# Per head means of squares of the sliding window attention's queries and keys: small fp32 matmuls and transposes, or two dense matmuls in split precision

## The chip, the cores and the metric

One core of a Trainium2 chip runs the whole program. The metric is the time of one execution on the device in microseconds; smaller is better.

## The reference, cut to what matters

A hybrid layer (gated linear attention beside sliding window attention, then a gated MLP) and two layers of another model follow each other on one sequence of 512 tokens with model width 1024. The change touches one step of the first layer: the RMS normalisation of each head's query and key in the sliding window attention, 8 query heads and 2 key heads of 64 elements.

```python
def rms_norm(x, g):
    xf = x.astype(jnp.float32)
    y = xf * lax.rsqrt(jnp.mean(xf * xf, axis=-1, keepdims=True) + EPS)
    return (y * g.astype(jnp.float32)).astype(x.dtype)
...
    h = rms_norm(x, mix_norm)
    z = h @ w_in
    gq, gk, gv, gr, glr, sq, sk, sv = split_cols(z, SPLITS)
...
    sq = rms_norm(sq.reshape(B, L, SWA_HEADS, SWA_HD), q_norm)
    sk = rms_norm(sk.reshape(B, L, SWA_KV_HEADS, SWA_HD), k_norm)
    sv = sv.reshape(B, L, SWA_KV_HEADS, SWA_HD)
    o_swa = swa_sink_attention(sq, sk, sv, sinks).astype(dt)
```

## The kernel before

Activations lie with the features on the 128 partitions and the 512 tokens along the free axis. Each engine has a program of its own, written out in order by hand; semaphores join them, and nothing reorders them.

**Split precision.** Every large product runs as fp32r matmuls on split operands. A weight tile of 128x1024 lands in `stage`; ScalarE copies it to `w_hi` (`split_hi`, called `split(t)`, L1346), GpSimd subtracts to get `w_lo` (`split_lo`, L422, four instructions of 128x256). TensorE then runs 24 matmuls of 128x512 into one of two PSUM banks: 16 with `w_hi` (against `xn_hi` and `xn_lo`), 8 with `w_lo` (against `xn_hi`). `stage`, `w_hi` and `w_lo` have two buffers each. ScalarE splits tile t + 2 in its round t; GpSimd's split of tile t + 1 waits for ScalarE's split of it (`hi_ready`) and for tile t - 1 on TensorE (`tile_done`).

**The input projection.** Tiles 0 to 3 are another form. Tiles 4 to 17 run in the loop `for t in range(N_GV, N_IN)` on TensorE: `dense(T_IN, t, a, b)` issues matmuls a to b of the 24, and `at_0`, `at_8`, `at_12` and `at_16` put other work between them (at the tile's start, after 8, after 12, after 16). VectorE and ScalarE have loops with the same t. VectorE's `project(t - 1)` (L2015) scales a finished tile out of its bank into `z`.

**The normalisation.** The five tiles that hold keys (index 0) and queries (1 to 4) are handled in rounds `SUMS_AT = [5, 6, 9, 11, 13]`. For index i: ScalarE squares the tile into `tmp` (`swn_square`, L1441). TensorE sums the squares by four fp32 matmuls with the squares as stationary operand and two columns of a constant as moving one (`swn_sums`, L716, at `at_12`), which gives 8 columns, tokens on the partitions. ScalarE takes Ln and Exp of the 8 columns (`swn_root`, L1446, L1447), VectorE makes a Newton step on them and spreads them to 128x512 (`swn_newton`, L2020 to L2023), TensorE transposes that back by four transposes (`swn_spread`, L724, at `at_0` of a later round), and VectorE multiplies the tile by it (`swn_scale`, L2029). `MB` is the PSUM bank all this goes through.

**What stands around it.** ScalarE's round 5 holds, after the root of index 0, the gate chain of the linear attention (L1551, L1552, L1554), then `split(7)`. Its round 6 holds square and root of index 1, `decays(0)`, `split(8)`. VectorE's round 6 holds `log_decay(0)` and `log_decay(1)`, each a tensor_tensor (L2033), a scan (L2035) and a tensor_tensor (L2038), all from SBUF. At `at_0(7)` TensorE makes tables from the bias (L831, L832). The queries' and keys' scores come at `at_16` of rounds 7, 8, 10 to 15 (L666), the attention's transposes at L678.

## Time and profile before

| | |
|---|---|
| median of 3 runs | 1754.53 us (1753.83 to 1754.73) |
| profiled execution, its own time | 1754.19 us |
| span of its trace | 1752.4 us |
| busy in the span | TensorE 1736.8, VectorE 826.6, ScalarE 751.9, GpSimd 979.3 us |
| mean granted clock of TensorE | 0.999 of full speed |

The span runs from the first to the last instruction of the trace; the execution's own time has 1.8 us around it. Times in the trace are counted from the span's start. Matmuls overlap, so the distance between the starts of two of them is what one costs, not its length.

### The profile page before, as it was taken

Reading aid. Unit: us, or ns where it says so; the run is one execution under the profiler, and the core shown is the slowest. Engines: PE = TensorE matmul, PEld = TensorE weight load, DVE = VectorE, ACT = ScalarE, POOL = GpSimd, SP = SyncE. Lnnn points to the kernel's source line nnn. Section 1 sums busy time; section 2 is a strip of 40 time slices with the busy share of each in tenths; the row PEclk is TensorE's granted clock in tenths of the full one; section 3 lists DMA queues with packets and bytes.
Section 4 is the critical chain, followed back from the end, with each engine's and each line's share of the span. In section 5 each row is a group of like instructions: output and inputs, shape, how many; then the busy total and the mean of one; then the engine's idle time right before and its main releaser. Section 6 shows DMA issues by size and latency. Waiting matters only on the chain.

```text
span 1752.4 us, 25481 instructions
## 1 busy us (share of the span) xinstructions
PE 1736.8 (99%) x8358; PEld 1413.3 (81%) x8358; DVE 826.6 (47%) x1611; ACT 751.9 (43%) x1226; POOL 979.3 (56%) x1176
## 2 busy tenths in 40 slices
PE   8999999999999999999999999999999999999998
PEld 6777788888888778888888888877777888888887
DVE  4764655555311455566232323567677551414143
ACT  4455555555322444435232323346565542323243
POOL 5433655555555434357575757755554675757574
PEclk9999999999999999999999999999999999999999
DMA  5221223332323322222232322323331333332232
GB/s 189 70 67 61 84 98 96 96 96 96 96 96 138 105 67 82 73 85 96 96 96 96 96 96 96 138 81 106 108 108 50 96 95 98 96 96 96 96 96 96
DMA packets 48484, 167.41 MB, mean 96 GB/s; under 512 B 5328, under 2 KB 6624, under 8 KB 48384
## 3 DMA queue, kind: packets, MB, share of 16 engines
q1 hardware_dynamic: 48032, 165.83, 29.1%
q8 instruction: 43, 0.70, 0.2%
q10 hardware_dynamic: 384, 0.67, 0.1%
q14 instruction: 25, 0.20, 0.0%
HBM read 164.24 MB, written 2.24 MB: 95 GB/s over the span
## 4 chain that ended last, share of the span: by engine, by line
PE 97%; ACT 1%; DVE 1%; issue 0%; DMA 0%; POOL 0%; SPq 0%; DVEq 0%; POOLq 0%; ACTq 0%
PE bank L620 19%; PE bank L518 13%; PE bank L519 13%; PE bank L524 13%; PE bank L928 5%; PE bank L929 5%; PE bank L933 5%; PE bank L971 2%; PE bank L977 2%; PE bank L972 2%; PE bank L638 2%; PE bank L639 2%; PE bank L644 2%; PE bank L1194 1%; PE bank L1223 1%; PE bank L1206 1%
## 5 line engine op out<-in xcount | busy, mean ns | idle before, releaser
L422 POOL TENSOR_TENSOR w_lo<-stage,w_hi 128x256 fp32r<-128x256 f32 x1128 | 926.3, 852 | 715.3 <-ACT w_hi L1346 408.5
L1346 ACT ACTIVATE w_hi<-stage 128x1024 fp32r<-128x1024 f32 x282 | 298.0, 1057 | 480.8 <-PE bank L519 337.6
L518 PE MATMUL bank<-xn_hi,w_hi 128*128 128x512 f32 x544 | 211.7, 389 | 0.0
L519 PE MATMUL bank<-xn_lo,w_hi 128*128 128x512 f32 x544 | 211.6, 389 | 0.0
L518 PE MATMUL bank<-arena,w_hi 128*128 128x512 f32 x496 | 192.9, 389 | 0.0
L519 PE MATMUL bank<-arena,w_hi 128*128 128x512 f32 x496 | 192.9, 389 | 0.0
L620 PE MATMUL bank<-xn_hi,w_hi 128*128 128x512 f32 x464 | 190.3, 410 | 0.0
L620 PE MATMUL bank<-xn_lo,w_hi 128*128 128x512 f32 x464 | 182.0, 392 | 0.0
L928 PE MATMUL bank<-xn_hi,w_hi 128*128 128x512 f32 x352 | 136.9, 389 | 0.0
L929 PE MATMUL bank<-xn_lo,w_hi 128*128 128x512 f32 x352 | 136.9, 389 | 0.0
L524 PE MATMUL bank<-xn_hi,w_lo 128*128 128x512 f32 x544 | 135.0, 389 | 0.0
L524 PE MATMUL bank<-arena,w_lo 128*128 128x512 f32 x496 | 132.6, 389 | 0.0
L1895 DVE TENSOR_TENSOR x<-x,bank 128x512 f32 x48 | 33.0, 688 | 210.8 <-PE bank L524 210.8
L2609 DVE TENSOR_TENSOR tmp<-tmp,rstd 128x512 f32<-128x512 f32 x64 | 46.0, 718 | 170.8 <-ACT tmp L1867 170.5
L620 PE MATMUL bank<-xn_hi,w_lo 128*128 128x512 f32 x464 | 123.7, 399 | 0.0
L519 PEld LDWEIGHTS bank<-xn_lo,w_hi 128*128 128x128 f32 x544 | 102.1, 188 | 21.2
L524 PEld LDWEIGHTS bank<-xn_hi,w_lo 128*128 128x128 f32 x544 | 102.1, 188 | 21.2
L518 PEld LDWEIGHTS bank<-xn_hi,w_hi 128*128 128x128 f32 x544 | 102.1, 188 | 21.1
L518 PEld LDWEIGHTS bank<-arena,w_hi 128*128 128x128 f32 x496 | 93.1, 188 | 19.4
L524 PEld LDWEIGHTS bank<-arena,w_lo 128*128 128x128 f32 x496 | 93.1, 188 | 19.3
L519 PEld LDWEIGHTS bank<-arena,w_hi 128*128 128x128 f32 x496 | 93.1, 188 | 19.3
L620 PEld LDWEIGHTS bank<-xn_hi,w_hi 128*128 128x128 f32 x464 | 87.2, 188 | 26.3 <-issue 9.9
(331 smaller groups left out, 2827.4 us busy)
## 6 DMA issues: line engine op xcount, KB each, us to landing
stage<-weights SPq DMA_DIRECT2D x283, 512.0 KB, 3.4
bias<-table SPq DMA_DIRECT2D x11, 896.0 KB, 5.3
out<-z SPq DMA_DIRECT2D x8, 256.0 KB, 2.1
x<-x_in SPq DMA_DIRECT2D x3, 512.0 KB, 7.8
bias<-swa_table SPq DMA_DIRECT2D x4, 256.0 KB, 4.5
con<-consts SPq DMA_DIRECT2D x1, 640.0 KB, 10.0
bias<-table SPq DMA_DIRECT2D x5, 128.0 KB, 3.5
stage<-weights ACTq DMA_DIRECT2D x2, 256.0 KB, 4.1
```

The lines of the kernel that those rows point to most:

```text
L422: ins = nc.gpsimd.tensor_tensor(w_lo[:, p_, ks], stage[:, p_, ks], w_hi[:, p_, ks].bitcast(F32), ALU.subtract)
L518: pe.matmul(G[p_][:], w_hi[:, p_, k], hi[:, k], start=(first and k == ks[0]), stop=False)
L519: mm = pe.matmul(G[p_][:], w_hi[:, p_, k], lo[:, k], start=False, stop=False)
L524: mm = pe.matmul(G[p_][:], w_lo[:, p_, k], hi[:, k], start=False, stop=(last and k == ks[-1]))
L620: mm = pe.matmul(G[p_][:], (w_hi if i < 2 * KD else w_lo)[:, p_, k], (xn_lo if i < 2 * KD and i % 2 else xn_hi)[:, k], start=(i == 0), sto ...
L638: pe.matmul(G[dd][:], w, ff_hi[:, k], start=(k == k0), stop=False)
L639: mm = pe.matmul(G[dd][:], w, ff_lo[:, k], start=False, stop=False)
L928: pe.matmul(UP[bank][:], w_hi[:, p_, k], xn_hi[:, k], start=(k == 0), stop=False)
L929: mm = pe.matmul(UP[bank][:], w_hi[:, p_, k], xn_lo[:, k], start=False, stop=False)
L933: mm = pe.matmul(UP[bank][:], w_lo[:, p_, k], xn_hi[:, k], start=False, stop=(k == KD - 1))
L1346: act.activation(w_hi[:, p_], stage[:, p_], ACT.Copy).then_inc(hi_ready, 1)
L2609: dve.tensor_tensor(tmp[:, 2 + p_], tmp[:, p_], rstd[:], ALU.mult).then_inc(u_ready, 1)
```

## The change

The sums go by two dense fp32r matmuls of 128x512 with a block diagonal matrix `mean_h` (1/64 within each head's 64 rows): the squares are split in a high part (ScalarE, Copy into `swn_split[:, 0]`) and a low part (GpSimd, `swn_low`), as in every large product. The result has the mean of each head already spread over its 64 partitions, so nothing is transposed. ScalarE's root works on 128x512 (Ln, Exp, and the square of the result), and the Newton step becomes part of VectorE's scaling, three operations of 128x512 in place of three small or spreading ones and one; the factor -0.5 goes into the norms' weights at the start. The pair of matmuls stands at `at_16`, where the sums stood at `at_12`. GpSimd's loop over tiles is written out, with `swn_low` behind the split of the next tile. The copy that makes `mean_r` moves to the opening. Cut to its core:

```diff
@@ -145,6 +145,7 @@
         mean_r = sb("mean_r", [P, P], F32R)
+        mean_h = sb("mean_h", [P, P], F32R)
@@ -154,6 +155,7 @@
         square_split = zr[:, 16:18]
+        swn_split = zr[:, 12:14]
         y = z[:, 0:KD].rearrange("p k s -> p (k s)").rearrange("p (h k s) -> p h k s", h=2, k=KD)
@@ -434,10 +435,18 @@
-            with pool.Fori(1, T_OUT // 2 + 1) as m:
-                for p_ in range(2):
-                    split_lo(m, p_)
-            split_lo(T_OUT // 2 + 1, 0)
+            def swn_low(i):
+
+                pool.wait_ge(swn_hi, i + 1)
+                if i:
+                    pool.wait_ge(swn_ss, i)
+                nc.gpsimd.tensor_tensor(swn_split[:, 1], tmp[:, i % 2], swn_split[:, 0].bitcast(F32),
+                                        ALU.subtract).then_inc(swn_lo, 1)
+
+            for t in range(2, T_OUT + 3):
+                split_lo(t // 2, t % 2)
+                if t - 1 in SUMS_AT:
+                    swn_low(SUMS_AT.index(t - 1))
             gla_low(0)
@@ -708,21 +717,14 @@
-            def swn_sums(i):
-
-                pe.wait_ge(swn_sq, i + 1)
+            def swn_means(i):
+
+                pe.wait_ge(mean_ready, 2)
                 pe.wait_ge(*((swn_done, i) if i else (rstd_ready, 1)))
-                for t in range(NQ):
-                    mm = pe.matmul(MB[:, 2 * t:2 * t + 2], tmp[:, i % 2, t * P:(t + 1) * P], ccol("mean_64")[:, 0::64],
-                                   start=True, stop=True)
-                mm.then_inc(swn_ss, 1)
-
-            def swn_spread(i):
-
-                pe.wait_ge(swn_found, i + 1)
-                for t in range(NQ):
-                    mm = pe.transpose(MB[:, t * P:(t + 1) * P], tmp[:, i % 2, t * P:(t + 1) * P], ident)
-                mm.then_inc(swn_turned, 1)
+                pe.wait_ge(swn_hi, i + 1)
+                pe.matmul(MB[:], mean_h[:], swn_split[:, 0], start=True, stop=False)
+                pe.wait_ge(swn_lo, i + 1)
+                pe.matmul(MB[:], mean_h[:], swn_split[:, 1], start=False, stop=True).then_inc(swn_ss, 1)
@@ -821,10 +823,7 @@
-                if t == 6:
-                    swn_spread(0)
-                elif t == 7:
-                    swn_spread(1)
+                if t == 7:
                     pe.wait_ge(buckets_in, 16)
@@ -835,14 +834,8 @@
                     token_major(1)
-                elif t == 10:
-                    swn_spread(2)
                 elif t == 11:
                     token_major(2)
-                elif t == 12:
-                    swn_spread(3)
-                elif t == 14:
-                    swn_spread(4)
                 if t in TURN_AT:
@@ -862,14 +855,14 @@
             def at_12(t):
-                if t in SUMS_AT:
-                    swn_sums(SUMS_AT.index(t))
                 if t == 16:
             def at_16(t):
+                if t in SUMS_AT:
+                    swn_means(SUMS_AT.index(t))
                 if t in TURN_AT:
@@ -1437,14 +1430,21 @@
                 if i >= 2:
-                    act.wait_ge(swn_turned, i - 1)
+                    act.wait_ge(swn_done, i - 1)
                 act.activation(tmp[:, i % 2], z[:, SWN_TILES[i]], ACT.Square).then_inc(swn_sq, 1)
+                act.wait_ge(swn_sq, i + 1)
+                if i:
+                    act.wait_ge(swn_ss, i)
+                act.activation(swn_split[:, 0], tmp[:, i % 2], ACT.Copy).then_inc(swn_hi, 1)
                 act.wait_ge(swn_ss, i + 1)
-                link("act", act, act.activation(swn_y, MB[:, 0:8], ACT.Ln, bias=eps_col))
-                act.activation(swn_y, swn_y, ACT.Exp, scale=-0.5).then_inc(swn_r, 1)
+                if i:
+                    act.wait_ge(swn_done, i)
+                link("act", act, act.activation(rstd_h[:], MB[:], ACT.Ln, bias=eps_col))
+                link("act", act, act.activation(rstd_h[:], rstd_h[:], ACT.Exp, scale=-0.5))
+                act.activation(tmp[:, i % 2], rstd_h[:], ACT.Square).then_inc(swn_r, 1)
@@ -1525,6 +1525,9 @@
             act.activation(glr_w[:, :, 0:16], pcol("w_glr").rearrange("p (k c) -> p k c", k=KD), ACT.Copy).then_inc(glr_split, 1)
+            act.wait_ge(con_in, 16)
+            act.activation(mean_r[:], ccol("mean_d"), ACT.Copy).then_inc(mean_ready, 1)
+            act.activation(mean_h[:], ccol("mean_64"), ACT.Copy).then_inc(mean_ready, 1)
             split(4)
@@ -1558,7 +1561,6 @@
                     act.activation(lam_s[:, 2:4], lam_s[:, 0:2], ACT.Exp).then_inc(lam_exp, 1)
-                    act.activation(mean_r[:], ccol("mean_d"), ACT.Copy).then_inc(mean_ready, 1)
                     act.wait_ge(tab_sb, 3)
@@ -2002,6 +2004,8 @@
                               glr_w[:, :, 0:16].bitcast(F32), ALU.subtract).then_inc(glr_split, 1)
+            both = par[:, _cols["q_norm"][0]:_cols["k_norm"][1]]
+            dlink(dve.tensor_scalar(both, both, -0.5, None, ALU.mult))
             dve.tensor_scalar(neg_sinks, pcol("sinks"), -1.0, None, ALU.mult).then_inc(sink_negated, 1)
@@ -2014,19 +2018,15 @@
-            def swn_newton(i):
+            def swn_scale(i):
                 dve.wait_ge(swn_r, i + 1)
-                dlink(dve.scalar_tensor_tensor(out=swn_a, in0=MB[:, 0:8], scalar=EPS, in1=swn_y, op0=ALU.add, op1=ALU.mult))
-                dlink(dve.scalar_tensor_tensor(out=swn_b, in0=swn_a, scalar=-0.5, in1=swn_y, op0=ALU.mult, op1=ALU.mult))
-                wide = [v.rearrange("p (g o) -> p g o", o=1).broadcast_to([P, 8, 64]) for v in (swn_b, swn_y)]
-                dve.scalar_tensor_tensor(out=tmp[:, i % 2].rearrange("p (g d) -> p g d", g=8), in0=wide[0], scalar=1.5, in1=wide[1],
-                                         op0=ALU.add, op1=ALU.mult).then_inc(swn_found, 1)
-
-            def swn_scale(i):
-                dve.wait_ge(swn_turned, i + 1)
                 zi, g = z[:, SWN_TILES[i]], pcol("q_norm" if i else "k_norm")
-                dve.scalar_tensor_tensor(out=zi, in0=zi, scalar=g, in1=MB[:], op0=ALU.mult, op1=ALU.mult).then_inc(swn_done, 1)
+                dve.scalar_tensor_tensor(out=zi, in0=zi, scalar=g, in1=rstd_h[:], op0=ALU.mult, op1=ALU.mult)
+                dlink(dve.scalar_tensor_tensor(out=tmp[:, i % 2], in0=MB[:], scalar=eps_col, in1=tmp[:, i % 2],
+                                               op0=ALU.add, op1=ALU.mult))
+                dve.scalar_tensor_tensor(out=zi, in0=tmp[:, i % 2], scalar=-3.0, in1=zi, op0=ALU.add,
+                                         op1=ALU.mult).then_inc(swn_done, 1)
@@ -2138,7 +2138,6 @@
                 if t == 5:
-                    swn_newton(0)
                     for j in range(2):
@@ -2146,7 +2145,6 @@
                     log_decay(0)
-                    swn_newton(1)
                     log_decay(1)
@@ -2176,8 +2174,6 @@
                     scale(SCORE_AT.index(t - 1))
-                if t in SUMS_AT[2:]:
-                    swn_newton(SUMS_AT.index(t))
                 if t in SCORE_AT:
```

TensorE in rounds 5 to 7 of the loop, before: the end of tile 6 and what follows. L620 are the tile's matmuls, L716 the sums, L724 the transposes, L831 and L832 the tables.

```order
L620 MATMUL bank<-xn_lo,w_hi 128x512
L716 MATMUL bank<-con,tmp 128x2 [waits swn_done,swn_sq]
L716 MATMUL bank<-con,tmp 128x2 x3
L620 MATMUL bank<-xn_hi,w_hi 128x512
L620 MATMUL bank<-xn_lo,w_hi 128x512
L620 MATMUL bank<-xn_hi,w_hi 128x512
L620 MATMUL bank<-xn_lo,w_hi 128x512
L620 MATMUL bank<-xn_hi,w_lo 128x512 [waits lo_ready]
L620 MATMUL bank<-xn_hi,w_lo 128x512 x7
L724 MATMUL bank<-con,tmp 128x128 [waits swn_found]
L724 MATMUL bank<-con,tmp 128x128 x3
L831 MATMUL bank<-ff_space,par 16x512 [waits gate_log,buckets_in]
```

The same place after (L629 are the tile's matmuls, L725 and L727 the new pair, L830 the tables):

```order
L629 MATMUL bank<-xn_hi,w_hi 128x512
L629 MATMUL bank<-xn_lo,w_hi 128x512
L725 MATMUL bank<-arena,mean_h 128x512 [waits swn_hi,swn_done,mean_ready]
L727 MATMUL bank<-arena,mean_h 128x512 [waits swn_lo]
L629 MATMUL bank<-xn_hi,w_lo 128x512 [waits lo_ready]
L629 MATMUL bank<-xn_hi,w_lo 128x512 x7
L830 MATMUL bank<-ff_space,par 16x512 [waits gate_log,buckets_in]
```

The pair stands after the sixteenth matmul and not after the twelfth, waits for a second engine, and the transposes are gone.

GpSimd after, from the w_lo split of tile 5 to that of tile 8 (L423 the splits, L443 the low part of the squares):

```order
L423 TENSOR_TENSOR w_lo<-stage,w_hi 128x256 x3
L423 TENSOR_TENSOR w_lo<-stage,w_hi 128x256 [waits tile_done,hi_ready]
L423 TENSOR_TENSOR w_lo<-stage,w_hi 128x256 x3
L443 TENSOR_TENSOR arena<-tmp,arena 128x512 [waits swn_hi]
L423 TENSOR_TENSOR w_lo<-stage,w_hi 128x256 [waits tile_done,hi_ready]
L423 TENSOR_TENSOR w_lo<-stage,w_hi 128x256 x3
L443 TENSOR_TENSOR arena<-tmp,arena 128x512 [waits swn_ss,swn_hi]
L423 TENSOR_TENSOR w_lo<-stage,w_hi 128x256 [waits tile_done,hi_ready]
```

Before, the same stretch was a loop of the splits alone; the two L443 are new, each behind the split of the tile that comes after the one whose pair needs it.

ScalarE before, from the root of index 0 to that of index 1 (L1346 is the w_hi split of tile 7):

```order
L1446 ACTIVATE small<-bank,small 128x8 [waits swn_ss]
L1447 ACTIVATE small<-small 128x8 [waits act_chain]
L1551 ACTIVATE qkv<-bank,par 128x512 [waits gate_abs,gate_in]
L1552 ACTIVATE qkv<-qkv 128x512 [waits act_chain]
L1551 ACTIVATE qkv<-bank,par 128x512 [waits gate_abs,gate_in,act_chain]
L1552 ACTIVATE qkv<-qkv 128x512 [waits act_chain]
L1554 ACTIVATE qkv<-qkv 128x512 [waits act_chain]
L1554 ACTIVATE qkv<-qkv 128x512
L1346 ACTIVATE w_hi<-stage 128x1024 [waits hi_free,stage_full1]
L1441 ACTIVATE tmp<-z 128x512 [waits evac1]
L1446 ACTIVATE small<-bank,small 128x8 [waits swn_ss]
```

The same after (L1445 to L1447 the root, L1339 the w_hi split, L1434 the square, L1438 its high part):

```order
L1445 ACTIVATE rstd_h<-bank,small 128x512 [waits swn_ss]
L1446 ACTIVATE rstd_h<-rstd_h 128x512 [waits act_chain]
L1447 ACTIVATE tmp<-rstd_h 128x512 [waits act_chain]
L1554 ACTIVATE qkv<-bank,par 128x512 [waits gate_abs,gate_in]
L1555 ACTIVATE qkv<-qkv 128x512 [waits act_chain]
L1554 ACTIVATE qkv<-bank,par 128x512 [waits gate_abs,gate_in,act_chain]
L1555 ACTIVATE qkv<-qkv 128x512 [waits act_chain]
L1557 ACTIVATE qkv<-qkv 128x512 [waits act_chain]
L1557 ACTIVATE qkv<-qkv 128x512
L1339 ACTIVATE w_hi<-stage 128x1024 [waits hi_free,stage_full1]
L1434 ACTIVATE tmp<-z 128x512 [waits evac1]
L1438 ACTIVATE arena<-tmp 128x512 [waits swn_ss,swn_sq]
```

The split of tile 7 still stands ahead of the square of index 1; the root ahead of the gate chain has grown from two small activations to three of 128x512.

## Rows read from the trace of the kernel before

**Rows 1.** Page, part 1: busy time, share and instructions of each engine.

```profile
PE 1736.8 (99%) x8358; PEld 1413.3 (81%) x8358; DVE 826.6 (47%) x1611; ACT 751.9 (43%) x1226; POOL 979.3 (56%) x1176
```

**Rows 2.** Page, part 4: the chain that ended last, by engine.

```profile
PE 97%; ACT 1%; DVE 1%; issue 0%; DMA 0%; POOL 0%; SPq 0%; DVEq 0%; POOLq 0%; ACTq 0%
```

**Rows 3.** Waits of TensorE: total us, times, longest.

```profile
PE bank L716 <- ACT tmp L1441: 0.5, 1, 0.5
```

**Rows 4.** Timeline, TensorE, tiles 5 and 10: start us, length us.

```profile
45.38 0.40 PE L620 MATMUL bank<-xn_lo,w_hi 128*128 128x512 f32 x1
...
46.73 0.39 PE L620 MATMUL bank<-xn_lo,w_hi 128*128 128x512 f32 x1
...
48.57 1.65 PE L620 MATMUL bank<-xn_hi,w_lo 128*128 128x512 f32 x6
...
84.42 0.60 PE L724 MATMUL bank<-con,tmp 128*128 128x128 f32 x4
84.86 0.60 PE L678 MATMUL bank<-con,prob 128*128 128x128 f32 x4
```

**Rows 5.** Timeline, TensorE, the pair with mean_r after the first layer's mixer.

```profile
217.08 0.39 PE L576 MATMUL bank<-arena,mean_r 128*128 128x512 f32 x1
...
217.54 0.40 PE L928 MATMUL bank<-xn_hi,w_hi 128*128 128x512 f32 x1
```

**Rows 6.** Timeline, ScalarE, from the gate chain on.

```profile
48.98 0.69 ACT L1551 ACTIVATE qkv<-bank,par 128x512 f32<-128x512 f32 x1 [1.88 <-DVE qkv L2145]
...
52.81 1.04 ACT L1346 ACTIVATE w_hi<-stage 128x1024 fp32r<-128x1024 f32 x1
53.76 0.61 ACT L1441 ACTIVATE tmp<-z 128x512 f32<-128x512 f32 x1
```

**Rows 7.** Timeline, GpSimd: w_lo splits of tiles 6, 7, 9 and 12.

```profile
41.86 2.80 POOL L422 TENSOR_TENSOR w_lo<-stage,w_hi 128x256 fp32r<-128x256 f32 x4 [5.83 <-PE bank L620]
53.93 3.50 POOL L422 TENSOR_TENSOR w_lo<-stage,w_hi 128x256 fp32r<-128x256 f32 x4 [9.27 <-ACT w_hi L1346]
...
67.97 3.73 POOL L422 TENSOR_TENSOR w_lo<-stage,w_hi 128x256 fp32r<-128x256 f32 x4 [5.08 <-PE bank L620]
...
93.61 2.83 POOL L422 TENSOR_TENSOR w_lo<-stage,w_hi 128x256 fp32r<-128x256 f32 x4 [5.62 <-PE bank L620]
```

**Rows 8.** Line 434, GpSimd, a 128x512 subtraction: ns min/median/max.

```profile
L434 POOL TENSOR_TENSOR arena<-z,arena x2: 1290/1292/1293, 171.0 to 172.3; 128x512 fp32r<-128x512 f32 x2
```

**Rows 9.** Timeline, VectorE, operations that meet GpSimd's splits.

```profile
52.42 0.69 DVE L2033 TENSOR_TENSOR qkv<-qkv 128x512 f32<-128x512 f32 x1 [0.35 <-ACT qkv L1554]
53.14 1.23 DVE L2035 TENSOR_TENSOR_SCAN qkv<-con,qkv 128x512 f32<-128x512 f32 x1
54.40 1.03 DVE L2038 TENSOR_TENSOR qkv<-qkv 128x512 f32<-128x512 f32 x1
...
69.08 0.88 DVE L2049 TENSOR_TENSOR qkv<-z,qkv 128x512 f32<-128x512 f32 x1
69.88 1.23 DVE L2051 TENSOR_TENSOR qkv<-z,qkv 128x512 f32<-128x512 f32 x1
```

**Rows 10.** Timeline, TensorE, tiles 6, 7 and 11.

```profile
56.37 2.00 PE L620 MATMUL bank<-xn_hi,w_lo 128*128 128x512 f32 x8
...
58.74 0.60 PE L831 MATMUL bank<-ff_space,par 32*16 32x512 f32 x1
...
98.47 0.70 PE L666 MATMUL bank<-z 64*128 64x256 f32 x4
```

**Rows 11.** Timeline, TensorE, its first matmuls.

```profile
6.91 2.07 PE L793 MATMUL bank<-w_hi,xn_hi 128*128 128x512 f32 x4 [6.91 <-ACT w_hi L1491]
...
10.48 1.30 PE L793 MATMUL bank<-w_hi,xn_hi 128*128 128x512 f32 x4
```

**Rows 12.** Windows at the run's end: us, busy of PE, PEld, DVE, ACT, POOL, PEclk, DMA.

```profile
1746.00:1748.00 2.00, 0.29 (x2) 0.00 (x0) 0.75 (x3) 1.20 (x3) 0.37 (x1) 1.00 0.83 318
1748.00:1750.00 2.00, 0.00 (x0) 0.00 (x0) 1.33 (x5) 0.00 (x0) 1.04 (x2) 0.58 0.56 218
```

More of the change, by code:

```diff
@@ L208, in program @@
         gla_queries, gla_x_ready = sem("gla_queries"), sem("gla_x_ready")
-        swn_sq, swn_ss, swn_turned, swn_done = sem("swn_sq"), sem("swn_ss"), sem("swn_turned"), sem("swn_done")
-        swn_found = sem("swn_found")
+        swn_sq, swn_ss, swn_done = sem("swn_sq"), sem("swn_ss"), sem("swn_done")
+        swn_hi, swn_lo = sem("swn_hi"), sem("swn_lo")
         gv_sum, gv_ln, gv_root, gv_ready = sem("gv_sum"), sem("gv_ln"), sem("gv_root"), sem("gv_ready")
@@ L297, in program @@
         swa_v = v_tok[:, 0, 0]
-        swn_y, swn_a, swn_b = (small[:, a:a + 8] for a in (24, 32, 40))
         neg_sinks = small[:, 56:64]
```

## The prediction

> **What bounds the kernel now.** I read the page's busy table first: TensorE has work for 1736.8 of 1752.4 us, VectorE, ScalarE and GpSimd for about half [rows 1]. The chain of work that ended last says the same, 97% of it is TensorE [rows 2], and the list of waits shows one wait of 0.5 us on TensorE in the stretch of the change, before the sums of squares of tile 6 [rows 3]. So an edit counts by what it takes from TensorE's stream, and by what it makes TensorE wait for. I call "tile t" the 24 matmuls of the t-th projection tile: 16 with w_hi, then 8 with w_lo. All clock times below are those of the profile of before; a shifted one is called "new".
>
> **What TensorE is rid of.** In tile 5 the last matmul ahead of the sums starts at 45.38, the second behind them at 46.73: 1.35 us for two steps [rows 4]. A plain step is (217.54 - 217.08) / 2 = 0.23 us [rows 5], so the four small matmuls cost 1.35 - 0.46 = 0.89 us. The four transposes run from 84.42 until the next group at 84.86 [rows 4]: 0.44 us. The two new dense matmuls have the form of those with mean_r, which take two steps: 0.46 us [rows 5]. Per normalised tile that is 0.89 + 0.44 - 0.46 = 0.87 us less, 4.35 us for all five if nothing waits.
>
> **Where it waits: tile 6.** The new pair stands behind the 16 w_hi matmuls, ahead of the w_lo ones, and everything behind it on TensorE stands still with it: the w_lo part of tile 6, the table matmuls, tile 7. The second of the pair needs a 128x512 subtraction on GpSimd, and GpSimd does it after the whole w_lo split of the next tile, which waits for ScalarE's w_hi split of that tile.
>
> TensorE's side: the w_lo part of tile 5 started at 48.57, new 48.57 - 0.89 + 0.46 = 48.14; 8 steps later tile 6 starts, new 49.98 (no transposes between), and 16 steps later TensorE is at the pair: new 53.7.
>
> ScalarE's side: its gate chain started at 48.98 and led to the w_hi split of tile 7 at 52.81, 1.04 long [rows 6]. In the new order it follows the pair of tile 5, which starts four steps after 45.61, ends at 46.53 + 0.23 + 0.39 = 47.15, and then three 128x512 activations, 0.69 for the one from PSUM and 0.61 for each of the others [rows 6], with some hundredths between: 49.1. That is 0.1 later than now, so the split ends at 53.96 and GpSimd starts at 54.04 (it started 0.08 behind ScalarE before, at 53.93 [rows 7]). The high part for the pair follows the split (Square 0.61, Copy 0.6): 55.2. It is not the last to come.
>
> GpSimd's side: undisturbed, a split takes 2.80 us [rows 7] and a 128x512 subtraction 1.29 [rows 8], 4.09 together: 58.1 at the earliest. But VectorE works on the log decays in just that time, and they read two operands from SBUF. Before, the scan ended at 54.37 and GpSimd's split then took until 57.43, 3.06 us, so one tensor_tensor behind the scan cost it 0.26; and it took 3.73 at 67.97 with two such operations at 69.08 and 69.88, 0.46 for each [rows 7, 9]. New, VectorE's scaling is three operations and not one, its decays come 0.55 later, and with the second head pair's decays following at once (no Newton step between) four operations fall into GpSimd's time behind the rest of the first scan: tensor_tensor, tensor_tensor, scan, tensor_tensor. Rest of the scan 54.93 - 54.04 = 0.89; then 0.26 + 0.46 + 0.8 + 0.46, where 0.8 for a scan is my choice between 0.46 and its whole 1.23. Sum 2.87. The low part is ready at 54.04 + 4.09 + 2.87 = 61.0. Bounds: 58.2 with no disturbance at all, and 62.3 if each operation holds GpSimd for its whole length (0.89 + 0.68 + 0.69 + 1.23 + 0.68 = 4.17; 0.69 is the undisturbed tensor_tensor [rows 9]).
>
> The Trainium skill (SBUF — State Buffer, "SBUF: two separate sides") says that GpSimd and a VectorE operation with two SBUF inputs take a shared port pair as an exclusive lock for a whole instruction. The trace agrees in part: the rest of a scan is paid whole, the rest less. By that rule the sum would end 1.3 us later; it is a rival below.
>
> So the w_lo part of tile 6 starts at 61.23, where it started at 56.37, and the table matmuls, which started at 58.74 with transposes of 0.44 ahead of them [rows 10], start at 61.23 + 2.37 - 0.44 = 63.16: **4.42 us later than now**. What is late next: ScalarE's root of tile 6, the w_hi split of tile 8 (about 66) and the tables (about 68.5). TensorE needs them at the w_lo part of tile 8 (76) and at the transposes ahead of it (72), so this lateness stays hidden.
>
> **Tiles 9 to 14.** Three pairs at 0.43 less and three groups of transposes at 0.44 less: -2.61 us. Here w_hi is there in time, and GpSimd starts at the tile's start. Tile 11 is tightest: its split runs 93.61 to 96.44 [rows 7], the subtraction ends at 97.73; TensorE is at the pair at 98.47 - 0.89 - 0.1 = 97.5 [rows 10] and at its second matmul at 97.7. I take 0.1 us of wait for all three. The bound is a split of 3.73 in each: 0.9 x 3 = 2.7.
>
> **The clock.** From new 54.0 to 61.0 TensorE has one matmul to do. At the end of the run it has 0.29 us of work in 1746 to 1748, and the granted clock, 1.00 there, is 0.58 in the next stretch with 0.50 as the level it falls to [rows 12]. That is a shorter rest than the new one, so I expect the fall from 2.4 to 1.2 GHz. Its price: after the wait at the start, eight matmuls take from 6.91 to 10.48, 0.446 each and not 0.23 [rows 11]: 1.8 us. Bounds: 0, and twice that.
>
> **Hidden edits.** ScalarE's copies of mean_r and mean_h and VectorE's one more tiny operation fall into the opening, where both wait for TensorE or the weights; ScalarE's larger root and one more copy a tile and VectorE's two more operations stand beside idle time, since both are busy for under half of the span [rows 1]. Without that cover they are about 2 us a tile on ScalarE, and late w_hi splits would be the first to show it. GpSimd's unrolled loop costs nothing that I can price from a row.
>
> **Sum**, against the profiled execution's 1754.19: +4.42 - 2.61 + 0.1 + 1.8 = +3.7, so 1757.9; that execution lies 0.3 under the median of the runs shown, so 1758.0.
>
> **The rivals.**
> - *The wait and the fall of the clock, as summed*: 1758.0, own range 1756.3 (scan and second decays hold GpSimd little) to 1760. Chance 0.48.
> - *The same wait, but the clock holds* (the matmul at 55.2 counts as work enough): 1756.2. Against it: 0.29 us of work did not hold it at the end. 0.15.
> - *GpSimd is hardly held up*: pair at 58.2, 2.8 us earlier, 1755.2, or 1753.4 with the clock held. Against it: 3.73 and 3.50 us in rows 7. 0.08.
> - *GpSimd is held for whole operations*: pair at 62.3, 1759.3. For it: the rest of the scan in rows 7 and 9. 0.16. This is the rule of the Trainium skill named above.
> - *Tiles 9, 11 and 13 wait too*, 0.9 each, since GpSimd's work there now meets VectorE's scaling of the probabilities: 1760.7. Against it: in time terms it is met only at its end. 0.08.
> - *On the other side, no wait in tile 6*: -4.35 and the 0.5 of rows 3: 1749.3. It would need the low part by new 53.9, so ScalarE's w_hi split of tile 7 about 6 us earlier than at 52.81; from a low part at about 58 on, no gain of 0.2% is left. 0.05.
>
> **The numbers.** No change can be told from one within 0.2%, 3.5 us: 1751.0 to 1758.0. The first case lies on that bound and gives about half to each side. Slower 0.46, same 0.49, faster 0.05. The range takes in the clock held with a middling wait below and whole operations with a dear clock above: 1754.0 to 1761.0.
>
> **What would show it.** Right: among TensorE's waits one of 5 to 6 us at the second mean_h matmul for GpSimd's subtraction near 61, one of about 1.2 at the first for ScalarE, none over 0.3 at the other four pairs; granted clock below 1.00 after 56 and for some us behind 61; matmul steps of 0.23 for the pairs; GpSimd's split at 54 taking 5 us or more. Wrong: a low part before 59, the clock at 1.00 throughout, waits in tiles 9 to 13, or ScalarE's w_hi splits late enough to stop TensorE in tiles 7 to 9.

## The result, and the profile of the changed kernel

The changed kernel is slower, but by less than half a per cent. Its five runs took 1758.42, 1759.58, 1762.48, 1763.05 and 1763.5 us, median 1762.48; the kernel before took 1753.83 to 1754.73, median 1754.33. The ratio is 1.004, 95% interval 1.0028 to 1.0051. The times lie in two groups. With the experiments that ran this kernel again there are 13 executions: seven at 1757.28 to 1759.58 (middle one 1758.25) and six at 1762.33 to 1763.5 (about 1762.7), none between. The prediction, 1758.0 with a range of 1754 to 1761, names the first group and misses the second. Three of the first five executions fell in the second group; of the six of run 1 below only two did, and their median is 1757.96. So which side of 1761 the median of a few executions lands on is chance; that there is a second group is not.

The profiled execution took 1758.42 us, of which 1756.6 are span. Part 1 of its page answers to [rows 1], the chain in part 4 to [rows 2]:

```profile
PE 1734.8 (99%) x8308; PEld 1409.7 (80%) x8308; DVE 833.2 (47%) x1607; ACT 761.4 (43%) x1237; POOL 985.3 (56%) x1181
...
PE 97%; POOL 1%; DVE 1%; ACT 1%; issue 0%; DMA 0%; SPq 0%; DVEq 0%; POOLq 0%; ACTq 0%
```

TensorE is busy for 2.0 us less and yet ends 4.2 us later. GpSimd is in the chain with 1% now. The waits of TensorE, which answer to [rows 3] (waited in total, times, longest), show why:

```profile
PE bank L727 <- POOL arena L443: 5.2, 1, 5.2
PE bank L725 <- ACT arena L1438: 1.4, 1, 1.4
```

L725 and L727 are the two matmuls of swn_means. Each waited once, for index 1, in tile 6. Here is TensorE's timeline there (start, length, idle before), which answers to [rows 10], and behind it the pair of index 3, the only other pair with any gap:

```profile
55.34 0.47 PE L725 MATMUL bank<-arena,mean_h 128*128 128x512 f32 x1 [1.38 <-ACT arena L1438]
61.05 0.79 PE L727 MATMUL bank<-arena,mean_h 128*128 128x512 f32 x1 [5.25 <-POOL arena L443]
61.64 3.61 PE L629 MATMUL bank<-xn_hi,w_lo 128*128 128x512 f32 x8
65.19 2.03 PE L830 MATMUL bank<-ff_space,par 32*16 32x512 f32 x4
...
71.41 0.93 PE L675 MATMUL bank<-z 64*128 64x128 f32 x8
...
103.20 0.40 PE L725 MATMUL bank<-arena,mean_h 128*128 128x512 f32 x1
103.56 0.50 PE L727 MATMUL bank<-arena,mean_h 128*128 128x512 f32 x1
```

The second matmul starts at 61.05 us. The eight w_lo matmuls behind it take 3.61 us, where they took 2.00 [rows 10]. GpSimd's and VectorE's timelines, which answer to [rows 7] and [rows 9]:

```profile
54.09 5.24 POOL L423 TENSOR_TENSOR w_lo<-stage,w_hi 128x256 fp32r<-128x256 f32 x4 [8.07 <-ACT w_hi L1339]
59.29 1.70 POOL L443 TENSOR_TENSOR arena<-tmp,arena 128x512 fp32r<-128x512 f32 x1
```

```profile
55.95 1.21 DVE L2033 TENSOR_TENSOR qkv<-qkv 128x512 f32<-128x512 f32 x1
57.19 1.63 DVE L2035 TENSOR_TENSOR_SCAN qkv<-con,qkv 128x512 f32<-128x512 f32 x1
```

The split takes 5.24 us, not 3.50, and the low part 1.70, not 1.29. VectorE's operations beside them are longer too: 1.21 and 1.63, where their like took 0.69 and 1.23. The granted clock is the column in front of the last two (DMA share and GB/s) of the windows:

```profile
58.50:59.00 0.50, 0.00 (x0) 0.00 (x0) 0.47 (x2) 0.00 (x0) 0.50 (x1) 0.69 0.00 0
...
65.00:65.50 0.50, 0.50 (x2) 0.12 (x2) 0.20 (x1) 0.50 (x3) 0.00 (x0) 0.50 0.00 0
65.50:66.00 0.50, 0.50 (x2) 0.09 (x1) 0.50 (x2) 0.50 (x2) 0.00 (x0) 0.98 0.00 0
```

It fell to 0.50 (1.2 GHz) at about 58.7 us and was back at 2.4 GHz at 65.5, 4.5 us after the work had begun again.

### The profile page after: what moved, and what is told of

Its sections match the earlier page's. It is cut to its first block, busy times and chain, and to the rows that moved or that the text cites. A ratio compares the mean times of both kernels' runs of the same rounds, so it can differ in the third digit from the quotient of the medians.

```text
span 1756.6 us, 25368 instructions
## 1 busy us (share of the span) xinstructions
PE 1734.8 (99%) x8308; PEld 1409.7 (80%) x8308; DVE 833.2 (47%) x1607; ACT 761.4 (43%) x1237; POOL 985.3 (56%) x1181
## 4 chain that ended last, share of the span: by engine, by line
PE 97%; POOL 1%; DVE 1%; ACT 1%; issue 0%; DMA 0%; SPq 0%; DVEq 0%; POOLq 0%; ACTq 0%
PE bank L629 19%; PE bank L527 13%; PE bank L533 13%; PE bank L528 13%; PE bank L926 5%; PE bank L921 5%; PE bank L922 5%; PE bank L965 2%; PE bank L964 2%; PE bank L970 2%; PE bank L647 2%; PE bank L648 2%; PE bank L653 2%; PE bank L1187 1%; PE bank L1216 1%; PE bank L1199 1%
## 5 line engine op out<-in xcount | busy, mean ns | idle before, releaser
L423 POOL TENSOR_TENSOR w_lo<-stage,w_hi 128x256 fp32r<-128x256 f32 x1128 | 925.6, 852 | 713.8 <-ACT w_hi L1339 433.2
L1339 ACT ACTIVATE w_hi<-stage 128x1024 fp32r<-128x1024 f32 x282 | 298.0, 1057 | 476.1 <-PE bank L528 336.1
L629 PE MATMUL bank<-xn_hi,w_hi 128*128 128x512 f32 x464 | 189.7, 409 | 0.0
L629 PE MATMUL bank<-xn_lo,w_hi 128*128 128x512 f32 x464 | 181.9, 392 | 0.0
L629 PE MATMUL bank<-xn_hi,w_lo 128*128 128x512 f32 x464 | 125.4, 403 | 0.0
L629 PEld LDWEIGHTS bank<-xn_hi,w_hi 128*128 128x128 f32 x464 | 87.2, 188 | 26.5 <-issue 9.9
```

The source lines that it names most:

```text
L423: ins = nc.gpsimd.tensor_tensor(w_lo[:, p_, ks], stage[:, p_, ks], w_hi[:, p_, ks].bitcast(F32), ALU.subtract)
L629: mm = pe.matmul(G[p_][:], (w_hi if i < 2 * KD else w_lo)[:, p_, k], (xn_lo if i < 2 * KD and i % 2 else xn_hi)[:, k], start=(i == 0), sto ...
L1339: act.activation(w_hi[:, p_], stage[:, p_], ACT.Copy).then_inc(hi_ready, 1)
```

## The experiments

Two measures serve throughout. One is **the base**: 1754.4 less the 4.35 us that the prediction took from TensorE's stream and the 0.5 us of wait in [rows 3], so 1749.55. A run should lie at the base plus its own waits plus what the clock costs. The sum is good to some 0.9 us only: the median of before was 1753.98 beside runs 5 to 8 and 1754.3 to 1754.4 elsewhere, and the opening of the program takes longer in one execution than in another (the first matmul of index 1's pair starts at 54.65 to 56.07 us in four profiles of the changed kernel). The other is **the stretch**: from the start of index 1's last matmul (L727 here) to tile 7's scores (L675). It holds the last matmul of the pair, the eight w_lo matmuls, the tables and 16 matmuls of tile 7. TensorE waits nowhere in it unless said, so its length tells the clock's cost. It is 71.41 - 61.05 = 10.36 us above.

**1. The same kernel again**, for the spread; no edit.

> The changed kernel, unaltered, for a second profiled execution and more times. The five timed executions lay between 1758.4 and 1763.5 us, and the profiled one was the fastest of them. Theory A (the clock): the executions differ in how long TensorE's clock stays at 1.2 GHz after the wait in tile 6. Then an execution that takes 1762 to 1763 us shows the same wait of 5.2 us at the second mean_h matmul, and a granted clock of 0.50 for 8 to 10 us longer than the 6.8 us (58.7 to 65.5) of the first profile; the time at half clock explains the whole difference at half its length. Theory B (a transfer or another wait differs): a slow execution shows a new or longer wait on TensorE elsewhere, and the clock back after some 7 us as in the first profile. If this profile falls on a fast execution, only the spread of the times counts.

Measured: 1757.28, 1757.54, 1757.66, 1758.25, 1762.33, 1762.6 us, ratio 1.003 (1.0018 to 1.0042). Both groups came again. The profiled execution is of the lower one: the same waits, stretch 10.26 us, clock down from 57.7 to 64.5.

**2. TensorE kept at work in the long wait.** Twenty useless matmuls between the two of the pair; the wait itself is left.

```diff
                 pe.matmul(MB[:], mean_h[:], swn_split[:, 0], start=True, stop=False)
+                if i == 1:
+                    for n in range(20):
+                        pe.matmul(SC[0][:], mean_h[:], xn_hi[:, n % KD], start=True, stop=True)
```

> The changed kernel with 20 dense 128x512 matmuls of no use issued between the first and the second matmul of the pair in tile 6, into a bank that is free there (steps of 0.23 us: 4.6 us, inside the wait of 5.2 us). The wait for GpSimd stays what it is, TensorE only isn't at rest in it. Theory A (the clock is what the wait costs beyond its length): no granted clock under 1.00 near tile 6, the second mean_h matmul starts at 61 as before, and the times fall to 1758.4 - 2.2 = 1756.2 us with a spread of under 1 us in place of 5. Theory B (the spread and the rest come from elsewhere): median 1762 and the spread stay. A third case: the extra matmuls end after the low part is ready and cost up to 1 us themselves.

Measured: 1756.19 us (1755.76 to 1757.11), ratio 1.0011 (1.0002 to 1.002). There is one group of times. TensorE's timeline, then the window in the middle of the extra work:

```profile
55.78 0.47 PE L725 MATMUL bank<-arena,mean_h 128*128 128x512 f32 x1 [1.38 <-ACT arena L1441]
56.09 4.83 PE L728 MATMUL bank<-xn_hi,mean_h 128*128 128x512 f32 x20
61.56 0.50 PE L730 MATMUL bank<-arena,mean_h 128*128 128x512 f32 x1 [0.64 <-POOL arena L443]
...
69.95 0.93 PE L675 MATMUL bank<-z 64*128 64x128 f32 x8
```

```profile
58.00:60.00 2.00, 2.00 (x10) 1.64 (x9) 1.97 (x2) 0.00 (x0) 2.00 (x3) 1.00 0.00 0
```

The pair still waits for GpSimd, until 5.78 us behind its first matmul, where it was 5.71. The clock stays at 1.00 and the stretch is 8.39 us. So the clock's cost is shown by taking it away: 10.36 - 8.39 = 2.0 us in the first profile, 1.9 in run 1's. The rest of the loss is the waits: 1749.55 + 1.38 + 5.25 = 1756.2, as measured.

**3. The table matmuls moved** behind the eighth matmul of tile 7.

```diff
             def at_0(t):
-                if t == 7:
-                    ...
-                elif t == 8:
+                if t == 8:
...
             def at_8(t):
+                if t == 7:
+                    make_tables()
```

> The changed kernel with the three table matmuls (32 rows by 16 columns of the array, 2.2 us at full clock) moved from the start of tile 7 to behind its eighth matmul, so that 16 full matmuls follow the wait in tile 6 without a break. Theory A1 (the clock comes back late because the thin table matmuls stand in the stretch behind the wait): median falls from 1762.5 towards 1758.4 and the spread narrows to 1 or 2 us. Theory A2 (how long the clock stays down is chance, whatever stands there): median stays within 1 us of 1762.5, spread of 5. The wait itself is the same in both.

Measured: 1758.98 us (1757.85 to 1759.81, 11 executions), ratio 1.0025 (1.0016 to 1.0034). The upper group is gone. The profiled execution has the waits unchanged, the clock down from 57.2 to 67.4 and a stretch of 10.91 us. That is what theory A1 said.

**4. High and low part earlier.** ScalarE makes index 1's square and high part ahead of the w_hi split of tile 7, and GpSimd its low part ahead of the w_lo split.

```diff
-                if t in SUMS_AT:
+                if t in SUMS_AT and t != 6:
                     swn_square(SUMS_AT.index(t))
...
+                if t == 5:
+                    swn_square(1)
                 split(t + 2)
...
                 split_lo(t // 2, t % 2)
-                if t - 1 in SUMS_AT:
+                if t - 1 in SUMS_AT and t != 7:
                     swn_low(SUMS_AT.index(t - 1))
+                if t == 6:
+                    swn_low(1)
```

> The changed kernel with index 1's square and high part moved on ScalarE ahead of the w_hi split of tile 7, and its low part on GpSimd ahead of the w_lo split of tile 7. Nothing else. My theory (the wait is GpSimd's low part standing behind a split that stands behind ScalarE's split): the second mean_h matmul of tile 6 starts at about 56.5 in place of 61.05, the rest on TensorE is two pieces of 0.5 and 2 us, the clock does not fall, and the time is 1751.5 to 1752.5 us, faster than before by 2 to 3 us. Rival (the clock falls at this shorter rest as well): the same start, but 1754 to 1758 us and a spread of some us. Rival (the w_lo split of tile 7 now comes too late): a new wait for w_lo in tile 7 takes some of it back.

Measured: 1751.65 us (1750.97 to 1753.59), ratio 0.9987 (0.9978 to 0.9996). With this order alone the change is a gain of 2.8 us and not a loss: the order decides the sign. TensorE's waits at the pair, and the clock in an execution that took 1753.24:

```profile
PE bank L729 <- POOL arena L443: 1.2, 1, 1.2
...
PE bank L727 <- ACT arena L1440: 0.4, 1, 0.4
```

```profile
56.00:56.50 0.50, 0.05 (x1) 0.05 (x1) 0.50 (x1) 0.00 (x0) 0.50 (x2) 1.00 0.00 0
56.50:57.00 0.50, 0.50 (x2) 0.41 (x3) 0.50 (x2) 0.00 (x0) 0.50 (x1) 0.57 0.00 0
...
59.50:60.00 0.50, 0.50 (x3) 0.33 (x1) 0.47 (x2) 0.50 (x2) 0.50 (x1) 0.52 0.00 0
```

The base and the two waits give 1751.2. In this execution even 1.6 us of waits was followed by a fall of 3.4 us (56.6 to 60.0), which began 0.1 us after TensorE was at work again; its stretch is 9.94 us, so the clock cost it 1.55. It is one of three at 1753.2 to 1753.6; the other eight lie at 1750.97 to 1752.07, where the sum without a fall is. That the clock held in them is likely, but no profile shows it.

**5. Run 4's edits, and the pair of index 1 behind the tables**, at the start of tile 7.

```diff
                     mm.then_inc(tab_mm, 1)
+                    swn_means(1)
...
-                if t in SUMS_AT:
+                if t in SUMS_AT and t != 6:
                     swn_means(SUMS_AT.index(t))
```

> As the run with index 1's high and low part made early (median 1751.65 us), and its pair of matmuls moved from behind the 16th matmul of tile 6 to behind the table matmuls at the start of tile 7. TensorE gets there at about 58, where the low part, ready at 56.5, is waiting. My theory: no wait over 0.3 us at any of the five pairs, the granted clock stays at 1.00, and the time is 1749.4 to 1750.2 us with a spread of about 1 us, which is before's 1754.4 less the 4.35 us that the five pairs save and less the wait of 0.5 to 0.8 that before had in tile 6. Rival: the scaling of index 1 is now late for the first scores in tile 7 (chance of a wait of 0.7 us there), or for the w_hi split of tile 8; then 1750.5 to 1752.

Measured: 1751.66 us (1751.04 to 1752.54), ratio 0.9987 (0.9978 to 0.9996). The rival came true. Tile 6 has no wait and the clock holds, but other waits stand in their place: 0.86 us at tile 7's scores for VectorE's scaling, 0.74 at tile 8's turn (the attention's transposes) for ScalarE, 0.57 at tile 9's pair for GpSimd. 1749.55 + 2.17 = 1751.7.

**6. VectorE's second log decay moved** behind the scaling of index 1, away from GpSimd's split.

```diff
                     log_decay(0)
-                    log_decay(1)
...
                     swn_scale(1)
+                    log_decay(1)
```

> The changed kernel with VectorE's second log decay (tensor_tensor, scan, tensor_tensor, all from SBUF) moved behind the scaling of index 1 in the next round, so that it does not meet GpSimd's work in tile 6. Theory (VectorE's two operand work holds GpSimd up by some 2.9 us, of which the second decay's three operations are 1.7): GpSimd's w_lo split of tile 7 takes about 4.0 us in place of 5.24, its low part 1.30 in place of 1.70, and the second matmul of the pair starts at 59.3 to 59.4 in place of 61.05; the faster group of times moves from 1757.3-1758.4 to 1755.6-1756.7. Rival (GpSimd is slow there for another reason, as its start behind ScalarE): 5.24 and 1.70 stay, and so does the time. A side effect: the tables are ready 3 us later on VectorE, for which TensorE has some 3 us of room.

Measured: 1759.62 us (1758.58 to 1759.91), ratio 1.003 (1.0019 to 1.0041). GpSimd and TensorE:

```profile
53.55 3.88 POOL L423 TENSOR_TENSOR w_lo<-stage,w_hi 128x256 fp32r<-128x256 f32 x4 [8.07 <-ACT w_hi L1339]
57.40 1.26 POOL L443 TENSOR_TENSOR arena<-tmp,arena 128x512 fp32r<-128x512 f32 x1
```

```profile
58.71 0.79 PE L727 MATMUL bank<-arena,mean_h 128*128 128x512 f32 x1 [3.44 <-POOL arena L443]
59.30 3.61 PE L629 MATMUL bank<-xn_hi,w_lo 128*128 128x512 f32 x8
62.84 3.59 PE L830 MATMUL bank<-ff_space,par 32*16 32x512 f32 x4
...
73.06 0.93 PE L675 MATMUL bank<-z 64*128 64x128 f32 x8
```

GpSimd's two pieces fell from 6.94 to 5.14 us, so VectorE's second decay had held it up by 1.8, and the wait fell by as much. The theory is right so far, but its time is 3 us off; nothing was gained, and against the lower group 1.4 us were lost: the clock was down from 57.8 to 71.5, the tables ran at half speed, and the stretch grew to 14.35 us, 6.0 above that of run 2, where the clock held.

**7 and 8. The changed kernel twice more**, one execution each, to catch a profile of the upper group; no edit.

> The changed kernel once more, one look, to catch an execution of the slower group (1762.3 to 1763.5 us in 5 of 11 executions so far; none when the table matmuls stood elsewhere, spread then 1757.9 to 1759.8). If it is one: the waits of TensorE are the same as in the fast group (1.4 and 5.2 us in tile 6), and the granted clock is 0.50 for some 10 us more than in the fast group's 6.8, through the table matmuls and tile 7, worth 5 us. Rival: a longer or another wait, the clock back after 7 us.

> The same as the look before it, for a second chance at an execution of the slower group: same waits, the clock down for some 10 us more.

Measured: 1758.3 and 1762.82 us. Run 7 is like the first profile (same waits, clock down from 58.8 to 65.6, stretch 10.50 us). Run 8 is of the upper group:

```profile
56.07 0.47 PE L725 MATMUL bank<-arena,mean_h 128*128 128x512 f32 x1 [1.38 <-ACT arena L1438]
61.79 0.80 PE L727 MATMUL bank<-arena,mean_h 128*128 128x512 f32 x1 [5.25 <-POOL arena L443]
62.38 3.61 PE L629 MATMUL bank<-xn_hi,w_lo 128*128 128x512 f32 x8
65.93 3.59 PE L830 MATMUL bank<-ff_space,par 32*16 32x512 f32 x4
...
75.95 0.93 PE L675 MATMUL bank<-z 64*128 64x128 f32 x8
```

```profile
56.00:58.00 2.00, 0.47 (x1) 0.19 (x1) 1.97 (x3) 0.00 (x0) 2.00 (x3) 0.77 0.01 4
...
66.00:68.00 2.00, 2.00 (x3) 0.34 (x4) 1.97 (x3) 2.00 (x5) 0.68 (x1) 0.50 0.00 0
...
72.00:74.00 2.00, 2.00 (x6) 1.52 (x6) 1.21 (x3) 0.00 (x0) 0.00 (x0) 0.50 0.57 229
74.00:76.00 2.00, 2.00 (x11) 1.39 (x9) 0.00 (x0) 0.00 (x0) 0.00 (x0) 0.96 0.45 74
```

The waits are the same to 0.01 us. The clock had not risen when the tables began, it stayed at 0.50 through them and came back at about 74.1, among tile 7's dense matmuls. The stretch is 14.16 us, 3.8 more than in the lower group; another 0.7 lies ahead of tile 6 (the pair starts at 56.07, not 55.34). Together 4.5: the distance of the two groups.

That 0.7 us is the opening. TensorE's steps there are slow at first, and in run 8 they stayed so for longer. Run 8, then the first profile:

```profile
10.43 1.91 PE L795 MATMUL bank<-w_hi,xn_hi 128*128 128x512 f32 x4
...
13.33 1.98 PE L805 MATMUL bank<-w_lo,xn_hi 128*128 128x512 f32 x8
```

```profile
10.62 1.22 PE L795 MATMUL bank<-w_hi,xn_hi 128*128 128x512 f32 x4
...
12.60 1.98 PE L805 MATMUL bank<-w_lo,xn_hi 128*128 128x512 f32 x8
```

The four matmuls of L795 take 1.71 us until the next group (at 12.14) in run 8, 0.43 each, and 1.06 (at 11.68) in the first profile.

**9. Early parts, and index 1's pair ahead of the tables**: run 5 with swn_means(1) one step sooner.

```diff
                 if t == 7:
+                    swn_means(1)
                     pe.wait_ge(buckets_in, 16)
```

> The kernel of the run before with the pair of index 1 one step earlier: behind the eight low matmuls of tile 6, but ahead of the six table matmuls. The squares still come early on ScalarE and GpSimd. Theory: the low part is there at 55.9 us and the lows end at 55.7, so the pair waits for under 0.3 us, TensorE has no rest and its clock stays at the full level; root and scaling of index 1 start 2.2 us sooner than with the pair behind the tables, so the 0.9 us of TensorE's wait for them in tile 7 goes, and the 0.7 and 0.6 us in tiles 8 and 9 shrink or go: 1749.4 to 1750.9 us, 1750.3 likeliest. Rival (what made tiles 8 and 9 wait is the later squares and splits of ScalarE and GpSimd and not the late scaling): only the 0.9 goes, 1750.6 to 1751.3. Rival that the gain of the early order is spent elsewhere: as before it, 1751.7.

Measured: 1752.13 us (1751.71 to 1753.17), ratio 0.9988 (0.9979 to 0.9997). All three waits of run 5 are still there (0.92, 0.74 and 0.58 us). VectorE, then TensorE's scores:

```profile
58.73 1.63 DVE L2040 TENSOR_TENSOR_SCAN qkv<-con,qkv 128x512 f32<-128x512 f32 x1
...
61.38 0.68 DVE L2024 TENSOR_TENSOR z<-bank,rstd 128x512 f32<-128x512 f32 x1
```

```profile
64.61 0.93 PE L677 MATMUL bank<-z 64*128 64x128 f32 x8 [0.92 <-DVE z L2033]
```

ScalarE's root ends at 59.6, so the scaling at 61.38 did not wait for it. VectorE itself is late: it works without a gap from 51.3 on, through the two log decays, whose operations are longer where GpSimd is at work beside them (1.21 and 1.63 us for 0.68 and 1.22). My expectation had the wrong engine.

**10. Runs 6 and 3 together**: second decays apart, and the tables behind the eighth matmul of tile 7.

> Two edits of earlier runs at once: the second log decay of VectorE behind the scaling of index 1 (which shortened the wait of the second matmul of tile 6's pair from 5.25 to 3.44 us, and yet gave 1759.6 us), and the six table matmuls behind the eighth matmul of tile 7, so that behind the wait nothing but matmuls over all 128 rows stands. Theory A (the thin table matmuls, 32 rows by 16 columns, keep the clock down when they come in the stretch in which it would rise, which is what took the gain of the shorter wait): with them out of the way the clock comes back some 3 to 6 us after the pair, not 12, and the time is 1755.5 to 1757.5 us. Theory B (the tables have no part, the clock comes back late for a reason of its own): the wait of 3.4 us stays, the clock is down over 10 us again, 1758.5 to 1760.

Measured: 1758.84 us (1758.42 to 1759.68), ratio 1.0026 (1.0016 to 1.0036). The clock's windows:

```profile
57.50:58.00 0.50, 0.00 (x0) 0.00 (x0) 0.00 (x0) 0.00 (x0) 0.50 (x2) 0.73 0.00 0
...
64.00:64.50 0.50, 0.50 (x2) 0.33 (x1) 0.50 (x2) 0.24 (x1) 0.18 (x1) 0.50 0.00 0
64.50:65.00 0.50, 0.50 (x4) 0.41 (x2) 0.50 (x1) 0.00 (x0) 0.50 (x1) 0.94 0.00 0
```

The clock fell when it did in run 6 (57.8), and the pair's second matmul came as in run 6 (58.79 against 58.71). With nothing else moved than the tables it was back at 64.6 and not at 71.5, and the stretch is 11.07 us, not 14.35. Runs 3 and 8 are a second such pair: the clock fell at 57.2 and 57.1 and TensorE began again at 61.95 and 61.79, and it was back at 67.4 with the tables moved, at 74.1 with them in place. So theory A's mechanism is shown; its time didn't come, and the measured one lies in theory B's range. Of the 3.3 us only 0.8 are seen in the median. About half of the rest went into two new waits (0.73 at tile 8's turn, 0.57 at tile 9's pair), where TensorE now arrives sooner. Both lead back to VectorE. Just ahead of the first, ScalarE waits for its `es`, a column of the attention's softmax:

```profile
81.63 0.20 ACT L1410 ACTIVATE es<-es 128x2 f32<-128x2 f32 x1 [3.59 <-DVE es L1956]
```

VectorE works without a gap from 63.0 us on, the moved decay for 3.5 us of it. That the waits would go without the move isn't shown: runs 5, 9 and 12 have the same two with the decay in its old place. 1749.55 + 1.38 + 3.45 + 1.30 + 2.68 of clock = 1758.4, the profiled execution's time.

**11. Without any low part.** It leaves out the low part of the squares for all indices.

```diff
-                pe.matmul(MB[:], mean_h[:], swn_split[:, 0], start=True, stop=False)
-                pe.wait_ge(swn_lo, i + 1)
-                pe.matmul(MB[:], mean_h[:], swn_split[:, 1], start=False, stop=True).then_inc(swn_ss, 1)
+                pe.matmul(MB[:], mean_h[:], swn_split[:, 0], start=True, stop=True).then_inc(swn_ss, 1)
```

> Leaves out the low part of the squares: GpSimd makes none and the pair is its first matmul alone, so the means are of squares rounded to the short format. Theory (the wait for GpSimd's low part behind its split of w_lo is where the change loses its time): the wait of 5.25 us in tile 6 is gone, that of 1.4 us for ScalarE stays, the clock holds or falls for no more than 3 us; from the 1756.2 us with a warm TensorE the 5.3 us and five second matmuls of 0.23 us go: 1749.7 to 1751.5 us, more by up to 1 where the clock falls. GpSimd's w_lo split of this tile stays 5.2 us long, since VectorE's decays beside it stay. Rival (the root and the scaling are the change's cost too and not only the low part): over 1753.

Measured: 1749.98 us (1749.23 to 1750.95), ratio 0.9976 (0.9966 to 0.9985), inside the range expected. The clock holds at 1.00 through tiles 6 and 7. The base less five matmuls of 0.23, plus the one wait of 1.42, gives 1749.8. GpSimd's w_lo split of tile 7 still takes 5.25 us: its slowness beside VectorE costs nothing by itself; it was dear because the low part stood behind it.

**12. One matmul in the long format for index 1**, on the squares themselves, behind tile 6's w_lo part; the others keep the pair.

```diff
+                if i == 1:
+                    pe.wait_ge(swn_sq, 2)
+                    pe.matmul(MB[:], mean_h[:].bitcast(F32), tmp[:, 1], start=True, stop=True).then_inc(swn_ss, 1)
+                    return
...
                 if t == 7:
+                    swn_means(1)
```

> For index 1 alone the pair becomes one matmul on the squares themselves, in the long format, behind the low matmuls of tile 6 and ahead of the tables; neither ScalarE nor GpSimd makes a part of these squares. The other four indices keep the pair. Its price is taken from the two table matmuls of 512 columns in the long format, 1.88 us together, so 0.94. Theory (what the change loses is the wait for index 1's parts in tile 6, and GpSimd's work for them, and nothing else): from the run without any low part, 1749.98, the wait of 1.42 us goes and so does its one matmul of 0.23, 0.94 comes in, and the four other second matmuls come back at 0.23 each: 1749.98 - 1.42 - 0.23 + 0.94 + 0.92 = 1750.2 us; the scaling of index 1 still starts behind VectorE's decays, so no new wait over 0.3 us in tiles 7 to 9, and the clock holds: 1749.7 to 1751.0. Rival (the scaling, now 0.75 us later beside TensorE's work, makes the scores of tile 7 and the turns of tile 8 wait as in the runs with early squares): 1751 to 1752. Rival (the long format takes far more than 0.94 us, or leaves the clock down): over 1752.

Measured: 1751.53 us (1751.09 to 1753.39), ratio 0.9985 (0.9976 to 0.9994). The time of the first rival came true, and half of what it said of the waits:

```profile
55.22 1.02 PE L726 MATMUL bank<-tmp,mean_h 128*128 128x512 f32 x2
...
62.32 0.93 PE L675 MATMUL bank<-z 64*128 64x128 f32 x8
...
75.73 0.63 PE L687 MATMUL bank<-con,prob 128*128 128x128 f32 x4 [0.74 <-ACT v_tok L1424]
...
79.03 0.50 PE L731 MATMUL bank<-arena,mean_h 128*128 128x512 f32 x1 [0.59 <-POOL arena L443]
```

The product costs what was said (0.95 us until the next group), the clock holds and tile 7's scores don't wait, but tiles 8 and 9 do, 1.33 us. TensorE is through tile 6 so early that VectorE, busy from 50 us past 76 without a gap, is the next to be late: ScalarE waits 3.57 us for VectorE's `es` ahead of the first of the two waits, and 0.72 us for VectorE's `z` ahead of the square that the second one needs. Runs 5, 9 and 12 reach the same 1751.5 to 1752.1 by three orders, and run 4 gets there with its waits in tile 6 instead.

## Why the prediction missed, step by step

The mechanism came as forecast: every sign that was to show it right is in the profile, and of those that were to show it wrong only 0.13 us of wait in tile 11. The step that failed is the size of one term, the clock's cost.

- **What TensorE is rid of, 4.35 us: right.** With it the base gives runs 2, 5, 11 and 12 within 0.2 us, run 9 within 0.4. The two traces say it directly for the last three pairs: the scores of tile 7 are 6.56 us later than before (71.41 against 64.85), those of tile 14 4.22 (137.99 against 133.77). The 2.34 us between, with 0.13 of wait, answer to the 2.61 of the sum.
- **The wait in tile 6: right.** The low part was forecast for 61.0, the second matmul came at 61.05; the waits were to be 1.2 and 5 to 6 us and were 1.38 and 5.25. GpSimd's two pieces took 2.85 us more than undisturbed (6.94 against 4.09 [rows 7, 8]), where the step had 2.87. Its 0.46 + 0.8 + 0.46 = 1.72 for the second decay is 1.8 in run 6.
- **Tiles 9 to 14: right**, 0.1 of wait forecast, 0.13 found.
- **Whole operations under an exclusive lock**, the rule of the Trainium skill (SBUF — State Buffer, "SBUF: two separate sides") and a rival with the pair at 62.3: the trace disagrees by 1.3 us. GpSimd lost 2.85 us beside VectorE and not the 4.17 of whole operations, and VectorE's operations got longer as well (1.21 for 0.69 us, 1.63 for 1.23).
- **The clock: right in kind, mis-sized.** This is the term that failed: "1.8 us. Bounds: 0, and twice that." It measured 2.0 us in the lower group, and 5.8 in the upper one (14.16 - 8.39), beyond the bound of 3.6. The step was sized well: at half clock the eight w_lo matmuls start 0.44 us apart, as in [rows 11]. What the term had wrong is how long it lasts. It let the clock come back after eight dense matmuls, as in the opening, the one place it was read from; in tile 6 the tables, 32 rows by 16 columns, stand behind the eight, and the clock that had not come back before them stayed down through them and for 3.8 us more (run 8). The sum with 5.8 and the 0.7 of the opening gives 1762.7.
- **The range** ended at 1761. Its upper end was the single clock price doubled with a dear wait, and had no case in which the clock isn't back when the tables begin. The sum itself has a slip of 0.2: 1757.9 with the 0.3 added is 1758.2.
- **The point of no gain.** The rival without a wait asked for the low part by 53.9 and said that no gain of 0.2% is left from about 58 on. By its own terms that point comes sooner: 0.2% under before is 1751.0, 1.5 us above the base, so a low part at about 55.4. Run 4, with the low part at 56.4, gains 2.8 us, which is 0.16%. The rival's 1749.3 was reached by no run that keeps the low part of every index; in runs 5, 9 and 12, which have no wait in tile 6, TensorE waits 1.3 to 2.2 us in tiles 7 to 9 behind VectorE.

**Open:** what sets the moment of the fall. With the program and the waits the same, it came at 57.1, 57.7, 58.7 and 58.8 us in four profiles. In the three of the lower group the clock was back before or just after the tables began (64.5, 65.5 and 65.6; tables from 64.51, 65.19 and 65.02), in that of the upper one it was not. That the clock stays down through the tables and comes back sooner without them is shown by runs 6 and 10, and 8 and 3; what shifts the moment is not. The rows have one lead: in the two profiles with the earliest fall among those with the full wait (runs 8 and 3, at 57.1 and 57.2) the slow steps of the opening also lasted longest, to 12.7 or 12.8 us, where they ended at 9.9 to 11.0 in the first profile and in runs 1 and 7 (estimates, from the time that each group of four matmuls takes until the next). Five profiles don't make it a rule. It is also only one profile that shows the upper group.

## What to carry over

When a product is split over two engines' results, look at what stands in front of the low part's instruction in its engine's queue: 1.3 us of GpSimd's work cost 5.25 us, since a split that nobody needed yet was ahead of it. A wait that TensorE spends idle can be paid twice, once by itself and once by the clock, and for the second read also what comes behind the wait: here the clock came back in dense matmuls, and stayed down through the small ones. Filling such a wait with useless matmuls tells the two prices apart in one run. When one kernel's times lie in two groups, take a profile of each before pricing anything.

## What was unexpected of the hardware

- The table matmuls kept TensorE busy without a gap for 4.4 us at 1.2 GHz, and the clock didn't come back in them; moved away, it came back 6.9 us sooner (run 10 against run 6).
- The same kernel has two groups of times, 4.5 us apart, with all waits equal: 3.8 us of it is the clock's return at 65.5 or at 74.1 us, and 0.7 the longer run of slow steps in the opening.
- The clock fell after short rests too: in one execution of run 4 at about 56.6 us, after waits of 0.44 and 1.20 us, and was back at 60.0. In run 11 a wait of 1.42 us left it at 1.00.
- The granted clock in the profile doesn't show everything: in the opening of every profile it reads 1.00, while the first 128x512 matmuls start 0.43 to 0.47 us apart; in tile 6, at 0.50, they start 0.44 us apart.
- GpSimd and VectorE slow each other down when both work from SBUF: a split of 2.80 us took 5.24, and 3.88 with one of the two decays moved away; a decay's tensor_tensor of 0.69 took 1.21 beside GpSimd's work.
